# Attention: the second part of the transposed probabilities leaves PSUM through VectorE instead of ScalarE

## The reference

```
def diff_combine(s, lam):
    p = jax.nn.softmax(s, axis=-1)
    return p[..., 0, :, :] - lam * p[..., 1, :, :]

def block(args):                       # one block of 128 query rows, all heads
    i, qi = args
    s = jnp.einsum('bqhmd,bkhmd->bhmqk', qi, k).astype(jnp.float32) * ATTN_SCALE
    s = jnp.where(k_pos[None, :] <= q_pos[:, None], s, NEG)
    attn = diff_combine(s, lam).astype(v.dtype)
    return jnp.einsum('bhqk,bkhe->bqhe', attn, v)
```

## Time and profile before

| | us |
|---|---|
| median of 3 runs | 3632.38 (3630.49 to 3639.15) |
| the profiled execution, its own time | 3636.3 |
| its span | 3634.5 |
| PE busy over the span | 3320.9 (91%) |
| DVE busy | 1898.3 (52%) |
| ACT busy | 1443.6 (40%) |
| POOL busy | 1761.4 (48%) |

### The profile page before, as it was taken

One profiled execution on the slowest core, in us unless ns is written; L12 is line 12 of the kernel. 1 busy time (PEld: TensorE's weight loads), 2 busy tenths in 40 slices (PEclk: granted clock), 3 DMA queues, 4 the chain that ended last, 5 costly groups with the idle time before them and its releaser, 6 DMA issues. The chain is left out here.

```text
span 3634.5 us, 78892 instructions
## 1 busy us (share of the span) xinstructions
PE 3320.9 (91%) x34073; PEld 3076.4 (85%) x34073; DVE 1898.3 (52%) x2173; ACT 1443.6 (40%) x2357; POOL 1761.4 (48%) x716
## 2 busy tenths in 40 slices
PE   7999958998997799999999999777887999999997
PEld 6798848888886799999999999654556999999997
DVE  6865464555555666573344332276645656741442
ACT  3333323343332344333333444365664443443342
POOL 3676600100010466666667666464303666766663
PEclk8999978999897899999999999888998999999998
DMA  8555543343343544445445576677755444444442
GB/s 289 155 170 174 156 150 117 114 139 123 118 127 115 179 137 137 140 139 155 140 145 149 155 207 186 185 236 275 267 168 181 136 135 142 139 143 140 139 144 85
DMA packets 784374, 575.21 MB, mean 158 GB/s; under 512 B 45290, under 2 KB 747522, under 8 KB 783772
## 3 DMA queue, kind: packets, MB, share of 16 engines
q1 hardware_dynamic: 728212, 506.00, 45.5%
q10 hardware_dynamic: 55816, 64.16, 5.4%
HBM read 499.80 MB, written 70.29 MB: 157 GB/s over the span
## 5 line engine op out<-in xcount | busy, mean ns | idle before, releaser
L1769 POOL TENSOR_TENSOR dense_w_lo<-w_raw,dense_w_hi 128x1024 fp32r<-128x1024 f32 x504 | 1291.6, 2568 | 916.0 <-ACT dense_w_hi L1852 915.8
L1821 PE MATMUL acc<-dense_x_hi,dense_w_hi 128*128 128x344 f32 x2496 | 793.1, 322 | 31.5 <-DVE dense_x_lo L1958 20.5
L1822 PE MATMUL acc<-dense_x_lo,dense_w_hi 128*128 128x344 f32 x2496 | 788.6, 321 | 0.0
L1852 ACT ACTIVATE dense_w_hi<-w_raw 128x1024 fp32r<-128x1024 f32 x504 | 530.8, 1056 | 509.7 <-PE acc L1826 446.3
L1821 PEld LDWEIGHTS acc<-dense_x_hi,dense_w_hi 128*128 128x128 f32 x2496 | 470.9, 189 | 37.9 <-DVE dense_x_lo L1958 16.2
L1821 PE MATMUL acc<-dense_hid_hi,dense_w_hi 128*128 128x344 f32 x1536 | 487.2, 322 | 0.0
L1822 PE MATMUL acc<-dense_hid_lo,dense_w_hi 128*128 128x344 f32 x1536 | 483.4, 319 | 0.0
L1822 PEld LDWEIGHTS acc<-dense_x_lo,dense_w_hi 128*128 128x128 f32 x2496 | 471.1, 189 | 0.6
L1826 PE MATMUL acc<-dense_x_hi,dense_w_lo 128*128 128x344 f32 x2496 | 447.8, 322 | 2.2 <-POOL dense_w_lo L1769 2.2
L1826 PEld LDWEIGHTS acc<-dense_x_hi,dense_w_lo 128*128 128x128 f32 x2496 | 407.6, 189 | 2.8 <-POOL dense_w_lo L1769 2.8
L864 POOL TENSOR_TENSOR x0T<-nT,levels 128x512 f32<-128x512 f32 x16 | 29.7, 1856 | 590.3 <-DVE bR L1534 590.3
(11 more groups left out here) (400 smaller groups left out, 5991.6 us busy)
## 6 DMA issues: line engine op xcount, KB each, us to landing
w_raw<-in_ffn_w SPq DMA_DIRECT2D x384, 512.0 KB, 4.2
proj_w_raw<-in_a_w_rkv SPq DMA_DIRECT2D x72, 512.0 KB, 4.2
att_k_page<-in_cache_k SPq DMA_DIRECT2D x64, 512.0 KB, 4.2
att_v_page<-in_cache_v SPq DMA_DIRECT2D x64, 512.0 KB, 5.8
w_raw<-in_ada_w SPq DMA_DIRECT2D x27, 1024.0 KB, 7.8
scratch_mix<-proj_stage ACTq DMA_DIRECT2D x72, 344.0 KB, 3.2
z<-scratch_mix SPq DMA_DIRECT2D x32, 512.0 KB, 9.1
ada_quarter<-in_ada_w SPq DMA_DIRECT2D x13, 1024.0 KB, 11.5
```

The costliest lines, as they stand in the source:

```text
L1769: nc.gpsimd.tensor_tensor(wlo[:, i % NW], raw[:, i % NRAW], whi[:, i % NW].bitcast(F32), ALU.subtract).then_inc(S("lo"), 1)
L1821: T_.matmul(out, whi[:, s % NW, k, :], a, start=j.first and k == 0, stop=False)
L1822: T_.matmul(out, whi[:, s % NW, k, :], b, start=False, stop=False)
L1852: A(whi[:, i % NW], raw[:, i % NRAW], ACT.Copy).then_inc(S("hi"), 1)
```

## The change

In every odd turn from 3 to 65, 32 in all, the copy of the second transposed part moves from ACT's list to DVE's. On ACT it stood between the two exponentials. On DVE it stands directly behind the maximum of the turn's new scores and ahead of the page sums and the combining. It keeps its waits (`t_mm`, `o_mm`) and still raises `t_in`.

```
--- before.py
+++ after.py
@@ -2490,6 +2490,12 @@
                 if u < NU:
                     maxima(u)
                 todo = list(pages_of(u))
+                second = attn_rounds(u - LAG)[1:]
+                for name in second:
+                    w = name[1]
+                    need(dve, "t_mm", nth[name] + 1)
+                    need(dve, "o_mm", w - 1)
+                    V.tensor_copy(aT[kind(w)][:, 4 * P:blocks(w) * P], tb[:, 0:(blocks(w) - 4) * P]).then_inc(S("t_in"), 1)
                 if todo:
                     page_sums(todo.pop(0))
                 if 1 <= u <= NU:
@@ -2638,7 +2644,7 @@
             for u in range(END):
                 w = u - LAG
                 for i in range(2):
-                    for name in attn_rounds(w)[i:i + 1]:
+                    for name in attn_rounds(w)[0:1] if i == 0 else []:
                         turned(name)
                     if 1 <= u <= NU:
                         exps(u - 1, (i,))
```

## The result

The changed kernel took 3640.91 us in the median of 20 runs (3632.48 to 3649.84), the kernel before 3633.81 (3614.67 to 3644.52, 20 runs) on the same chip. The ratio is 1.0022 [1.0014, 1.0030], which is 8 us slower. So the two measurements put the cost at 4 to 8 us of 3633, and only the first is clear of nothing by itself; 3640.1 was predicted.

The account below looks back on a forecast made before the run. No engine is full; chains of waits, including TensorE's on the one bank `tb`, make the time. Turn by turn the terms sum to 7.7 us, 3632.4 + 7.7 = 3640.1 us; range for 8 in 10: 3630 to 3652.

Parts of the forecast that it names:

- The cost of a copy: VectorE's copies of 512, 384, 256 and 128 columns take 0.69, 0.56, 0.42 and 0.29 us; TensorE starts 0.06 us later.
- behind GpSimd: Rival: each copy waits for GpSimd's product and moves the page sum; 10 us more, 3650 us; chance 0.06.
- Turns 3 to 23: Early turns: no cost; copies fit VectorE's wait for GpSimd, TensorE's slack absorbs getting the bank up to 2 us later.
- Turn 27: Largest term, +3.1 us: behind VectorE's slow sum of turn 26 TensorE gets the bank late, delaying turn 29's maximum.
- Turn 29: -1.0 us: TensorE gains its 1.33 us wait for ScalarE's second copy, limited by VectorE's normalising before turn 30's output transposes.
- Turns 33 and 35: +1.5 us: turn 33 loses 4.2 us at the bank, counted as nothing; turn 35's 1.5 holds, since page products follow.
- Turns 31, 39, 47 and 55: +0.8 us each, 3.1 in all: the copy behind a 1.23 us maximum makes TensorE's output transposes late.
- Turn 43: +1.5 us: TensorE starts at 2603.33 against 2601.86; it goes through, as VectorE is idle 5.86 us next turn.
- Turn 61: -1.2 us: TensorE no longer waits 1.24 us for the second copy, with no normalising in its way.
- By the clock: Rival: TensorE falls to the low clock behind new idle in turns 27, 33, 35, 43; 6 us, 3646; chance 0.22.
- All covered: Rival: TensorE's delays in turns 25 to 41 vanish in the VectorE and GpSimd loop; 3634 us; chance 0.17.
- Faster: Rival: ScalarE's relief decides, exponentials end 0.2 to 0.5 us earlier; 3624 us; chance 0.07.

Follow-up runs that it names:

- e1: Changed kernel with the copy on VectorE only in turns 3 to 23, ScalarE keeping the others: 3633.30 us, ratio 1.0006 to the kernel before.
- e10: Changed kernel with the copy on VectorE only in turns 3 to 23, each made twice: 3631.63 us against 3631.77 before, ratio 1.0003.
- e12: The changed kernel, unchanged, measured and profiled once more: 3635.17 us, ratio 1.0012 [0.9998, 1.0025] to the kernel before.
- e8: Changed kernel with the copy on VectorE in turn 27 alone: 3635.72 us against 3631.77 before, ratio 1.0010.
- e5: Changed kernel, but ScalarE keeps the copy in turns 25, 27, 33 and 35: 3634.03 us against 3631.23 before, ratio 1.0007.
- e11: The kernel before, unchanged, measured and profiled once more: 3632.62 us against 3632.85, ratio 1.0004 [0.9989, 1.0019].
- e7: Changed kernel with no copy on VectorE; ScalarE makes it behind both exponentials: 3653.66 us against 3631.23 before, ratio 1.0066.
- e6: Changed kernel with the copy ahead of the maximum on VectorE: 3636.04 us against 3631.23 before, ratio 1.0009.
- e4: Changed kernel with the copy on VectorE only in the eight turns 5, 13, 21, ... 61: 3633.08 us, ratio 1.0002 to the kernel before.
- e9: Changed kernel with the copy ahead of the maximum, ScalarE keeping turns 27 and 33: 3632.97 us against 3631.77 before, ratio 1.0002.

## Why the prediction was right, and where its terms were off

**The sign and the size: right, and in part by luck.** 3640.1 was predicted and 3640.9 measured, 7.7 us against 4.4 and 8.0 by the two ratios. The traces give 4.6 us between the pair whose clocks are alike in turns 50 to 55 and 10.8 between the other. The stage, from its first to its last combined block, grew by 10.4 and 5.3 us where 8 were forecast. Some terms below were counted and don't last, others were left out, and that the sum comes this close to the measured time is more than its terms warrant. (The range of the first case stands twice in the prediction, as 3638 to 3644 and as 3634 to 3646; the time is inside both.)

**The cost of a copy: right**, to 0.01 us in all four sizes, beside GpSimd's work as without it (turn 27 with POOL at work 0.67, turn 51 without 0.69). TensorE started 0.14 us behind the copy and not 0.06, but the copy started 0.07 us before the maximum had ended, so that the two nearly cancel. The rival "behind GpSimd" is dead: the copies lasted neither 2 us nor did they wait for the product.

**Turns 3 to 23: right.** e1 and e10 have no loss that the times can show, and at turn 24 their traces stand 1.0 us earlier and 0.7 us later than before, where 11 copies on the path would be 5.5 us. In turn 7 TensorE's wait grew from 0.49 to 3.05 us, so its values came 2.6 us later, where up to 2 were forecast. That cost 1.2 us in the one execution where the low clock followed and nothing in e12.

**Turn 25: right**, +0.7 in both pairs. **Turn 27: the delay is right, the +3.2 and +3.3 of the table are another sum.** The bank came 3.1 us later. Without the low clock (e8) that makes turn 28 only 0.6 us later, because VectorE didn't wait for TensorE before it, and turn 29 the other 2.5; the prediction had named the maximum of turn 29. In the changed kernel turn 28 carries the 0.6 and 2.6 of low clock, and turn 29 the 2.5 behind it. So turns 26 to 29 lose 5.6 and 6.0 us, of which 3.1 are the delay that was counted and the rest is the clock. e5 takes the whole step away. The backlog of turn 26 is the cause: the 2.34 us sum lies ahead of a copy that ScalarE would have made long before.

**Turn 29: the gain came, the stretch didn't show it.** TensorE's 1.33 us for the second copy are gone in the changed kernel:

```profile
2517.69 0.56 DVE L2498 COPY att_attn_cols_long<-aux 128x384 f32<-128x384 f32 x1 [0.45 <-PE aux L2299]
...
2518.40 0.63 PE L2299 MATMUL aux<-ident,att_v 128*128 128x128 f32 x4
...
2520.78 1.95 PE L2381 MATMUL aux<-att_fold,att_page_o 128*128 128x1 f32 x16 [1.09 <-ACT att_v_rows L2573]
```

But with the copy out of the way, the page columns wait 1.09 us for ScalarE's copy of the v rows. These columns start 6.3 us after those of before (2514.46 there), and the maximum of turn 29 6.7 us: 0.4 of the 1.33 us are left. Up to the maximum of turn 30 the gain is 0.9 us, of which 0.5 are scores that ran in 1.64 us instead of 2.14. So the size was met with another limit than the one forecast, and the table's +1.6 is this -0.9 and the 2.5 of turn 27's delay that reaches VectorE only in turn 29.

**Turns 33 and 35: half right.** In turn 33 TensorE waited 2.31 us at 2545.93 for the copy (about 4 were forecast), and it cost nothing, as said. In turn 35 the transposes came 6.73 us after those of before and VectorE's maximum 5.26, so the 1.5 us are there:

```profile
2556.44 0.68 DVE L2468 TENSOR_REDUCE att_neg_max<-acc 128x2 f32<-128x512 f32 x1
...
2557.04 0.68 DVE L2498 COPY att_attn_cols_long<-aux 128x512 f32<-128x512 f32 x1
...
2557.86 0.63 PE L2299 MATMUL aux<-ident,att_k 128*128 128x128 f32 x4 [1.01 <-DVE att_attn_cols_long L2498]
```

They reach turn 37 (+1.4 in both kernels after), and there they are given back: turn 37 gains 1.0 and 1.3 us instead of 0.4. The step that failed is "which holds, since page products follow". A late bank holds only until the next place at which TensorE isn't last.

**Turns 31, 39, 47 and 55, +0.8 each: wrong for the first three.** TensorE's transposes of the output did come some 0.8 us later in turn 31 (2531.39, 1.70 us behind the maximum at 2529.69; in the earlier trace rows it is 0.94). But from turn 31 to 32 the changed kernel took 6.25 us and the one before 6.43, and from 38 to 40 both pairs show 0.0. Here GpSimd is still at work, and VectorE's page sums and combining, not the scores, are what the next maximum waits for: there is no idle time in front of it in the trace before. In turns 47 and 55, without pages, it is idle there. In turn 55 the term shows: +0.8 to turn 56 in both pairs, and 0.0 between e11 and before. In turn 47, the one that was worked out, it doesn't: from turn 46 to 48 the pairs show +0.2 and 0.0. The output's transposes stand 8.39 us behind the maximum of turn 46 before and 8.54 after, 8.43 in e11 and 8.42 in e12, since each of the four had part of that turn's scores or values at the low clock (scores 2.08 and values 1.06 us before, 1.52 and 1.85 in e11), and the time from the one to the other came out alike. So two steps failed. "The other three look the same" held up to TensorE, and not one instruction further. And the 0.94 us of the earlier trace rows came from one trace in which the values ran at the full clock.

**Turn 43, +1.5: the delay is real, the clock hid it in one pair.** The k transposes came at 2609.06, 7.20 us after those of before, and VectorE's maximum 5.73. In turn 44 the scores took 1.56 us after and 2.88 before, and nothing was left of the delay (-0.1). In e12 and e11 they took 2.52 and 2.43 us, and turn 44 came 1.0 us later. First e11, then e12:

```profile
2598.54 2.43 PE L2317 MATMUL acc<-att_k,att_q 64*128 64x512 f32 x8
...
2601.62 1.76 DVE L2468 TENSOR_REDUCE att_neg_max<-acc 128x2 f32<-128x1536 f32 x1 [5.51 <-PE acc L2321]
```

```profile
2598.13 2.52 PE L2317 MATMUL acc<-att_k,att_q 64*128 64x512 f32 x8
...
2601.30 1.76 DVE L2468 TENSOR_REDUCE att_neg_max<-acc 128x2 f32<-128x1536 f32 x1 [6.66 <-PE acc L2321]
```

**Turn 61, -1.2: a part of it.** From turn 61 to 62 the trace after gains 1.4 us, e12 against e11 0.4; e11 itself gains 1.1 against before there. The values' second part waits no longer, but the next scores wait 0.84 us for ScalarE's exponentials at 2732.24. What the last row of the table has on top of it comes from the scores of turn 60, 2.88 us after and 1.56 before.

So the sum was near, and not every term was: 2.3 us of turns 31, 39 and 47 and most of turn 35's were counted and don't last, and a low clock behind TensorE's longer waits was left out.

**The rivals.** "By the clock" named a real effect, of 2.6 us in turns 27 and 28 of both executions of the changed kernel, and the wrong size for the whole. From the maximum of turn 25 to that of turn 44 the granted clock was 0.90 before and 0.90 after, 0.87 in e11 and 0.86 in e12 (below 0.87 was the sign that the prediction gave for this rival). TensorE was busy 106.1 and 106.4 us there, 110.3 and 110.9 in the second pair, while the stretch grew by 5.3 and 4.0 us. So the growth there is nearly all time in which TensorE waits, and what the low clock took in one turn it gave back in others. "All covered" is refuted by turns 25 to 29, where no delay vanished, and comes close from 38 on. "Faster" is refuted by the time itself; the exponentials do end 0.37 us earlier (turn 29), and in e7, where they do so too, the later bank outweighs it.

**Open.** How much of the 4.4 to 8.0 us is clock over the whole stage. Where the low clock falls differs between executions of one kernel and moves this stage by 4 to 5 us, more than the terms in dispute, and an experiment that holds it fixed wasn't found.

## What to carry to other kernels

When a resource with one slot, such as a single PSUM bank, is released by an engine, the engine's busy share (here VectorE at 44 to 75%) is not the question. Read what it has in its list at the moment of release: one copy of 0.7 us behind a backlog of 2.3 us made TensorE 3.1 us late, and the 11 copies of turns 3 to 23, in front of a wait, cost nothing that times or traces can show. A delay of TensorE counts only if the next instruction that waits for it was waiting already, so follow each to the next turn before adding it up. And for changes of 0.1 to 0.3% take a second profile of the same kernel before reading a difference between two traces as an effect.

## What the hardware showed beyond that

- Two executions of one kernel differ by up to 3.7 us in a stretch of 34 us with the same matmuls, by TensorE's granted clock alone (0.90 and 0.82).
- After a wait of 3 to 3.6 us TensorE ran at 1.2 GHz in some executions (turn 7 of after, turn 27 of after and e12) and at 2.4 in others (turn 7 of e12, turn 27 of e6 and e8).
- VectorE's copy out of PSUM takes 0.67 us for 512 columns beside GpSimd (turn 27 of the changed kernel) and 0.69 without it (turn 51), while its sum over 32 numbers in SBUF takes 2.34 us beside GpSimd (turn 26) and 0.17 without (turn 47).
- Ahead of the stage, where the code is the same in every kernel here, the profiled executions differ by up to 21 us: the maximum of turn 2 starts between 2329.4 us (e4) and 2350.5 (e9).
